# Eight row products per layer moved from beside the first table's late panels to the second table's first panels

## The reference, cut to what matters

```
eidx = ...                                # 128 expert numbers of each token
ue   = u_tab[eidx]                        # rows of the first table
a    = gelu(einsum('thkd,td->thk', ue, xt))
ve   = v_tab[eidx]                        # rows of the second table
y    = einsum('thk,thkd->td', g * a, ve)
```

## Time and profile before

| | us |
|---|---|
| median of 3 runs | 3677.57 |
| the profiled execution's own time | 3675.55 |
| its span, first to last instruction | 3673.8 |
| TensorE busy | 3544.4 (96%) |
| VectorE busy | 2482.3 (68%) |
| ScalarE busy | 1462.9 (40%) |
| GpSimd busy | 886.9 (24%) |
| mean granted TensorE clock | 0.985 of 2.4 GHz |

### The profile page before, as it was taken

The page is one execution under the profiler, slowest core; times in us unless marked ns, Lnnn a source line. Parts: engine busy times, 40 slices in busy tenths (PEclk is TensorE's granted clock), DMA queues, the critical chain, the costliest instruction groups (busy, mean ns, idle before and its releaser), DMA issues.

```text
span 3673.8 us, 54030 instructions
## 1 busy us (share of the span) xinstructions
PE 3544.4 (96%) x18308; PEld 2970.0 (81%) x18308; DVE 2482.3 (68%) x4635; ACT 1462.9 (40%) x2536; POOL 886.9 (24%) x1027
## 2 busy tenths in 40 slices
PE   5999999999999899999989999999999998999998
PEld 3777779999999777777667776999999997777775
DVE  6454678888888765555464556788888878655554
ACT  3323233334777333223243332333367753322232
POOL 0010100004333434444300010000053344344442
PEclk8999999999999999999999999999999999999999
DMA  7343334448999989999744433444499999899995
GB/s 254 124 169 124 133 119 149 149 149 284 342 339 344 380 306 342 350 342 353 272 145 153 142 114 128 143 150 146 148 323 349 337 361 355 308 347 352 345 344 188
DMA packets 269525, 909.67 MB, mean 248 GB/s; under 512 B 32212, under 2 KB 65028, under 8 KB 268452
## 3 DMA queue, kind: packets, MB, share of 16 engines
q0 software_dynamic: 126496, 473.44, 35.7%
q1 hardware_dynamic: 105984, 383.83, 30.0%
q10 hardware_dynamic: 36868, 50.35, 3.8%
HBM read 792.14 MB, written 115.34 MB: 247 GB/s over the span
## 4 chain that ended last, share of the span: by engine, by line
PE 91%; DVE 4%; DMA 3%; issue 1%; ACT 1%; POOL 0%; ACTq 0%; SPq 0%; DVEq 0%; POOLq 0%
PE ps L455 15%; PE ps L457 15%; PE ps L456 15%; PE ps L953 10%; PE ps L955 10%; PE ps L954 10%; PE ps L933 5%; PE ps L967 3%; PE ps L773 2%; DMA urow<-in_u_rows,idu 1%; PE ps L849 1%; PE ps L829 1%; PE ps L868 1%; PE ps L476 1%; DMA mod<-in_w_mod 1%
## 5 line engine op out<-in xcount | busy, mean ns | idle before, releaser
L455 PE MATMUL ps<-mov,whl 128*128 128x384 f32 (+1 forms) x2880 | 1045.2, 363 | 61.9 <-DVE whl L442 43.3
L457 PE MATMUL ps<-mov,whl 128*128 128x384 f32 (+1 forms) x2880 | 1016.6, 353 | 0.0
L456 PE MATMUL ps<-mov,whl 128*128 128x384 f32 (+1 forms) x2880 | 1014.7, 352 | 0.0
L442 DVE TENSOR_TENSOR whl<-raw,whl 128x1024 fp32r<-128x1024 f32 x648 | 792.6, 1223 | 211.9 <-ACT whl L432 207.8
L432 ACT CAST whl<-raw 128x1024 fp32r<-128x1024 f32 x648 | 680.0, 1050 | 108.6 <-ACT hst L1140 79.1
L455 PEld LDWEIGHTS ps<-mov,whl 128*128 128x128 f32 x2880 | 544.1, 189 | 122.0 <-issue 56.9
L953 PE MATMUL ps<-whl,wgthl 128*128 128x512 f32 x1536 | 617.7, 402 | 24.6 <-DVE wgthl L1631 24.4
L955 PE MATMUL ps<-whl,wgthl 128*128 128x512 f32 x1536 | 610.7, 398 | 0.0
L954 PE MATMUL ps<-whl,wgthl 128*128 128x512 f32 x1536 | 610.0, 397 | 0.0
L664 POOL DMA_INDIRECT urow<-in_u_rows,idu x256 | 303.6, 1186 | 1231.5 <-DVE idu L1564 785.9
L457 PEld LDWEIGHTS ps<-mov,whl 128*128 128x128 f32 x2880 | 543.8, 189 | 35.5
(11 more groups left out here) (239 smaller groups left out, 3539.0 us busy)
## 6 DMA issues: line engine op xcount, KB each, us to landing
raw<-in_uT_tab SPq DMA_DIRECT2D x256, 512.0 KB, 4.0
raw<-in_v_tab SPq DMA_DIRECT2D x256, 512.0 KB, 6.1
expert_spill<-hst ACTq DMA_DIRECT2D x256, 192.0 KB
hin<-expert_spill POOLq DMA_DIRECT2D x256, 192.0 KB, 5.8
gt<-weight_spill POOLq DMA_DIRECT2D x64, 768.0 KB, 7.4
weight_spill<-stage POOLq DMA_DIRECT2D x22, 2048.0 KB, 14.8
raw<-in_w_in SPq DMA_DIRECT2D x72, 512.0 KB, 4.5
raw<-in_w_mod SPq DMA_DIRECT2D x64, 512.0 KB, 3.7
```

Source lines behind the costliest of these rows:

```text
L442: nc.vector.tensor_tensor(whl[:, m % RING, 1], raw[:, raw_n(m) % RAW], whl[:, m % RING, 0].bitcast(F32), ALU.subtract).then_inc(lo_done, 1)
L455: nc.tensor.matmul(o, w[:, 0, k], src[:, 0, k, :cols], start=(k == 0), stop=False)
L456: nc.tensor.matmul(o, w[:, 0, k], src[:, 1, k, :cols], start=False, stop=False)
L457: mm = nc.tensor.matmul(o, w[:, 1, k], src[:, 0, k, :cols], start=False, stop=(k == KC - 1))
```

## The change

Row products per panel, by stage:

| | before | after |
|---|---|---|
| R1, 8 panels | 2 each: 16 | 0, 0, then 2 each: 12 |
| G, 48 panels | 1, 2, 1, 2, ...: 72 | the same |
| R2, 8 panels | 2 each: 16 | 2 each, then 0, 0: 12 |
| V, first 24 panels | 1 each: 24 | 1, 1, 2, 1, 1, 2, ...: 32 |

The gathers follow, since POOL reads the same function. `DOTS_V` is 24 in both.

```diff
 LATE_U = 2 * REST + NTB * BLK_U
 DOTS_V = 24
+DOTS = [0, 0] + [2] * (REST - 2) + [1, 2] * (N_G // 2) + [2] * (REST - 2) + [0, 0] + [1, 1, 2] * (DOTS_V // 3)
 
 
 def dots_by(p):
 
-    if p < REST:
-        return 2 * (p + 1)
-    if p < REST + N_G:
-        return 2 * REST + 3 * (p - REST + 1) // 2
-    if p < LATE_U:
-        return 2 * REST + 3 * N_G // 2 + 2 * (p - REST - N_G + 1)
-    return 4 * REST + 3 * N_G // 2 + min(p - LATE_U + 1, DOTS_V)
+    return sum(DOTS[:p + 1])
```

## The result

The changed kernel takes 3652.46 us (median of 4 runs, 3649.28 to 3654.7) against 3676.9 for the kernel before beside it; the ratio is 0.9937 (95% interval 0.9922 to 0.9952). Run once more beside its parts it took 3651.89, ratio 0.9937 (0.9923 to 0.9951). Forecast were 3650.5 us, and 26.8 us gained; 24.4 came.

A forecast was written before the change was run, and what follows sets the result against it. TensorE, 91% of the span, was taken as the bound, so only its idle or slow-clock time counts. R1's 17.7 and V's start's 9.1 make 26.8 us, all else 0: 3650.5 us forecast, range 3645 to 3662.

The forecast's parts named there:

- The account: R1: TensorE's idle before the fifth panel and the slow clock behind it go, 8.8 and 8.9 us per layer.
- The upper bound: R1: gain of 17.7 us over both layers, taken over the lower bound 12.2 since nothing idles TensorE there.
- Product times hardly move in absolute terms: R1: DVE does products when their rows land, as before, so POOL's gathers start when they did.
- No new wait: G's entry: first step's one-hot tiles placed at about 884, wanted by TensorE at 890.4; cost 0.
- R2 and V's start: V's start: four products of 1.14 us fewer ahead of the low part, 9.1 us over both layers.
- until R2's sixth panel nothing is changed: R2: same products per panel and same loads up to there, so the late rows are as late.
- the rest of the hole: V's start: 7.9 us stay, owned by rows awaited in R2's sixth panel and `weight(0)` behind them.
- The sum of 384 GB/s: V: transfer rate with 4/3 gathers per panel, 1.62 MB in 4.21 us, up from 342 GB/s.
- (a): Rival in V: transfers become the bound, 5 us per layer, 3660.5 us in all; chance 0.08.
- (c): Rival in R1: the hole only moves to the sixth panel's `split_lo`; with (b) 3677.6 us; chance 0.04.
- (d): Rival in V: the ring of six row buffers sets the pace, 19 us per layer, 3689 us; chance 0.05.
- (b): Rival in V: its start gives back 9 us, in panel 4's load or the next late thing; 3660; chance 0.07.

The follow-up runs named there:

- e4: Changed kernel with products 0 and 1 back beside R1's second panel, V 30: 3660.17 us, ratio 0.9962 to the kernel before.
- The mended version: e7 with R1's products 0, 0, 2, 2, 2, 2, 1, 1 and G 80, its doubles in the middle: 3631.59 us, ratio 0.9885.
- its two successors: The mended version with the first weight group's load ahead of three `hin` loads (3630.67 us, 0.9883); then also no products in R2, G 86 (3630.67 us, 0.9880).
- e2: Kernel before with only R2's part of the change: no products beside R2's last two panels, 28 in V: 3666.97 us, ratio 0.9976.
- e3: Kernel before with 32 products in V, the 8 more taken from G, R1 and R2 unchanged: 3676.46 us, ratio 1.0003.
- e6: Changed kernel with G 64 and V 40, two in each of V's first 16 panels: 3670.04 us, ratio 0.9983 to the kernel before.
- e7: e5 with the second weight group's load started five panels later: 3643.08 us, ratio 0.9910; its profiled execution 3630.47 us.
- e0: The changed kernel unaltered, run and profiled again: 3651.89 us, ratio 0.9937 to the kernel before.
- e5: Changed kernel with the 6 products of R2's fourth to sixth panel moved to G: 3641.24 us, ratio 0.9900 to the kernel before.

## Why the prediction was right

*R1.* The account held in size: 8.8 and 8.8 us for 8.8 and 8.9. The stand and the slow stretch behind it went together. With products 0 and 1 back (e4) the stand returns in both layers, and the slow stretch only behind the longer one of 3.13 us. The upper bound, that nothing idles TensorE any more there, was right up to G's first small matmuls.

One step of it was wrong without harm. "Product times hardly move in absolute terms" holds for the first two products. The third starts 12.4 us after the row numbers where it was 10.7 (11.9 for 11.0 in the second layer), since its row lands later; why, no run shows. So the seventh panel's `split_lo`, put "at worst" at 875.4, ends at 876.0 on the same base, and 0.8 us are left of the 1.4 to when TensorE wants it.

*G's entry: the step that failed.* "No new wait" there was wrong, by 0.8 to 1.3 us per layer. I looked at the one-hot tiles of G's first step only. Those of the second are made behind R1's eighth panel's two products, and ScalarE still has to scale them for 2.45 us. Before, they were ready 1.6 us ahead of TensorE. TensorE comes to G 8.8 us earlier, and in the first layer DVE comes to this tile only 6.0 us earlier: 39.7 us after the row numbers before, 33.7 after the change. Before, then after:

```profile
899.72 1.22 DVE L1586 TENSOR_TENSOR hotg<-sel1T,iota 128x1024 f32<-128x1024 f32 x1
```

```profile
895.87 1.22 DVE L1581 TENSOR_TENSOR hotg<-sel1T,iota 128x1024 f32<-128x1024 f32 x1
```

The mended version and its two successors, without the stand, show that it is this tile's wait. e2, with its R1 as before, had 0.57 us of the same wait in one layer, where DVE came to this tile 41.8 us after the row numbers instead of 39.7; so the margin of 1.6 us could be used up without the change, too. The next late thing is found by walking on from each engine's time, not from one tile.

*R2 and V's start.* 4.0 to 4.9 us for 4.6. The four products skipped, at 1.14 each, account for it within 0.6 us. The match is in part luck: the hole itself shrank by 5.0 to 5.1 us, and 0.1 to 1.1 of that went into a longer stand before R2's last panel, which I had taken as unchanged ("until R2's sixth panel nothing is changed"). That the rest of the hole belongs to the rows awaited in R2's sixth panel was true, but hid a second owner: with them gone, the first group's load takes their place.

*V.* The eight more products cost next to nothing beside the matmuls of the first 24 panels (e3). The sum of 384 GB/s was a little low: at the place that it started from, 386 to 398 were measured. The stretch from V's first matmul to `x_sb` is 0.7 to 1.8 us longer, and it was forecast at 0, with up to 1 us more for the slow clock. Two things add up to it in the second profile: V's first panel, run partly at the lower clock, ends 1.2 us and 0.05 us later behind its start than before, and a short wait of TensorE for a late `hin` load, there before with 0.1 us in the first layer, is 0.8 and 0.6 us long. In the second layer 0.3 us stay open. That load stands behind the eight row gathers of the second table, where the changed products have ended; why it is later I did not try.

*The limit on memory bandwidth.* The Trainium skill's "DMA: Bandwidth & Descriptors", section Specifications, gives a limit of about 358 GB/s of memory bandwidth per core, half of a figure for two cores. The changed kernel moved 398 and 385 GB/s over 60 us with TensorE never waiting, and e6 405 over 44 us. For this program on one core the measurement decides against the limit; what two cores at work get, no run here shows.

*The rivals.* (a), (c) and (d) did not come. (b), the load for V's panel 4, came near: POOL really waits now for the last `expert_spill` write, 7.62 us, but TensorE didn't feel it.

## What to carry to other kernels

When an engine's list mixes work that feeds the bottleneck with work that doesn't, look at what stands behind each wait, not at the wait: here 35 of 42 us of DVE's waiting for rows stayed, and 24 us of time went. Spare work belongs where the engine has slack on both sides of a stage's edge; in this kernel the first panels behind freshly started gathers and the last ahead of a stage that needs a new operand were the costly places. After a hole is closed, walk every engine's list one stage on: the engine that stood comes to the next edge earlier by the whole gain, and those that feed it by less (here 8.8 us against 6.0).

## What the runs showed of the hardware that I had not expected

A single stand of TensorE of 0.80 us (e7) or 2.04 us (e4) left the granted clock at 1.00. One of 3.13 us (e4), 3.31 us (e7) or more was followed by a stretch at 0.50, the 1.2 GHz level. In e4 that stretch cost 1.8 us: R1's first-layer stretch is 5.0 us longer with a hole of 3.13. Several short stands close together can do it as well: in e6's second layer the level fell behind stands of 1.09, 0.19 and 1.82 us, while in its first layer it stayed behind 0.78 and 1.76 us. What decides between these stays open. So a hole of a little over 3 us costs, as an estimate from e4, about 1.6 times its length.

And two loads of 768 KB issued at about the same place landed after 16.0 and 17.7 us in the change (e0, first layer) but after 21.5 and 23.1 in e5 (second layer: 16.5 and 18.0 against 20.0 and 22.1). The loads of `hin` ahead of them were later, too, 16.4 to 17.9 us against 13.1 to 14.5. e5 has two products in each of G's last twelve panels, and so more gathers just ahead; that these are the reason isn't shown.
